# Latent attention: two heads' scores per step, banks by use, and another order in the output projection

## The chip, the core and the metric

The kernel runs on one core of one Trainium2 chip. The metric is the device time in microseconds (us) of one execution of the whole program, lower is better. Engines are named as in the profile: PE (TensorE, matrix products; PEld are its weight loads), DVE (VectorE), ACT (ScalarE), POOL (GpSimd) and SP (SyncE, which here only issues DMAs). Each engine runs its own instructions in the order in which the program gives them and waits on semaphores for the others.

## What is computed

Two blocks follow one another on 512 tokens of width 1024. The first (convolution, stick-breaking attention, gated feed-forward) is not touched. The second has two layers of this form:

```python
for l in range(DEPTH):                                   # DEPTH = 2
    z = rmsnorm(x, norm_g[l]) @ w_in[l]                  # split into the parts of both mixers
    o_gla = gla_mix(...) * silu(g_gate)                  # 4 heads x 128, chunked gated linear attention
    q = (rmsnorm(c_q) @ w_uq[l]).reshape(B, S, 4, 192)   # 128 plain + 64 rotary values per head
    kv = (rmsnorm(c_kv) @ w_ukv[l]).reshape(B, S, 4, 256)
    q, k = rmsnorm per head, rotary on the last 64       # k's rotary part is one for all heads
    o_mla = block_causal_attention(q, k, v) * silu(m_gate)
    x = x + concat([o_gla, o_mla]) @ w_out[l]
```

`block_causal_attention` takes blocks of 128 queries: scores of block i over the keys up to its end, the causal mask on the diagonal block, softmax, product with the values. So for each of 4 heads there are 4 query blocks, with 128, 256, 384 and 512 keys.

## The kernel before

Everything is kept with features on the partitions and tokens along the free dimension: `X` is the residual in 8 blocks of 128 features by 512 tokens. A product with a weight matrix is made of blocks of 128x128 (`block`, L446 is the `mm` inside): each is three passes of 512 columns, high weights by high input, high by low, low by high (`XH`, `XL` are the two parts of an input, `wh`, `wl` those of the weights). `weight_order` writes out the order in which PE uses all weight blocks; they come in units of 8, which SP loads into `wraw`, ACT rounds to `wh` (L1096) and DVE completes with `wl` (L1686). The calls of `feed` and `feed_group` put this work into the queues of ACT and DVE, three units ahead of PE.

The order of all engines is written out by hand. In each layer of the second block, after the values (`by_token`, copied from banks 4 to 7 to `gv` by ACT), PE runs the attention mixed with the first pass of the output projection. Bank numbers are those of PSUM, 8 banks of 128x512.

- `att_scores(j)`, j = 4 * head + query block, on PE: a product with 128 rows (`qraw`, `kraw`; in the trace `bank<-states,gq` or `gk`), one with 64 rows for the rotary part (`qr`, `krh`; in the trace `bank<-krh,eb`), both in fp32, each two passes in the trace, and a mask (`identb`, `mml`). Head parity decides which half of the rows the rotary part uses. DVE takes the negated maximum (L2352) and scales it; ACT makes Exp with its sum (`tmp<-bank,sm,vr`); DVE takes the reciprocal (L2357) and scales the row (L1681).
- `att_turn(j)`: PE transposes the normalised row, 1 to 4 transposes (L1059); ACT copies the result to `PT`.
- `att_out(h)`: PE multiplies the values of head h by `PT` (`bank<-PT,gv`, 8 passes); DVE multiplies by the gate (`tmp<-bank,gates`), ACT and DVE make `XH`, `XL` of it: inputs 4 to 7 of the output projection.
- `halves()`: a generator, the first pass of the output projection. For each of 8 column blocks c it runs inputs 0 to 3; a step is two inputs (6 passes of 512 columns); on DVE, with the second step of c, the sum in the bank is added to `X[c]` (semaphore `out_a`). All engines go through the same generator.

The loop over j = 0 to 18 runs `att_scores(j)`, from j = 6 at every fourth step `att_out`, then `att_turn(j - 2)`, then one step of `halves`. `TURNS` lists scores and turns in their order; both rotate through banks 0 to 3, `att_out` uses banks 6 and 7, `halves` banks 4 and 5 by turns. The queues of ACT and DVE have the same loop.

After it comes the second pass: for each c inputs 4 to 7 (`out_a` and `at_t` free the banks), DVE adds to `X[c]` (`xsum`). In layer 0 ACT and DVE at once prepare the next layer's input from it, in layer 1 SP stores each `X[c]`.

Of the kernel before, what the change touches and what calls it, by code (L numbers as in the profile page):

```python
# [5 lines left out]
ALU = mybir.AluOpType  # L6
# [7 lines left out]
S = 512  # L14
D = 1024
KD = 8
# [29 lines left out]
def weight_order():  # L46
# [29 lines left out]
    for layer in range(2):  # L76
# [12 lines left out]
        o += [(f"out{layer}", k, c) for c in range(8) for k in range(4, KD)]  # L89
# [202 lines left out]
def place(nc, ctx, m):  # L292
# [86 lines left out]
    m.qr, m.kr = m.eb, m.kpb  # L379
    m.qraw = [m.gq[:, 0, :], m.gq[:, 1, :], m.gk[:, 0, :], m.gk[:, 1, :]]  # L380
# [8 lines left out]
TURNS = [("s", 0), ("s", 1)] + [x for j in range(2, 18) for x in ([("s", j)] if j < 16 else []) + [("t", j - 2)]]  # L389
# [52 lines left out]
def tensor_program(pe, m, s, w):  # L442
# [340 lines left out]
    for layer in range(2):  # L783
# [235 lines left out]
        def halves():  # L1019
            for c in range(8):  # L1020
                if c >= 2:
                    pe.wait_ge(s.out_a, 8 * layer + c - 1)
                else:
                    pe.wait_ge(s.gv, 8 * layer + 6)
                for k in range(4):
                    pe.wait_ge(s.mt, 8 * layer + k + 1)
                    block("out" + L, k, c, bank[4 + c % 2][:, :], XH[:, k, :], XL[:, k, :], k == 0, k == 3)
                    if k % 2:
                        yield

        side = halves()
        def free(n):

            if n >= 4:
                kind, j = TURNS[n - 4]
                pe.wait_ge(s.at_p if kind == "s" else s.at_t, 16 * layer + j + 1)
            else:
                pe.wait_ge(s.gate_r, 8 * layer + 8)

        def att_scores(j):  # L1040
            h, qb = j // 4, j % 4
            r = slice(64 * (h % 2), 64 * (h % 2) + 64)
            n, qs = 128 * (qb + 1), slice(qb * 128, qb * 128 + 128)
            t = TURNS.index(("s", j))
            o = bank[t % 4]
            free(t)
            mm(o[:, 0:n], m.qraw[h][:, qs], m.kraw[h][:, 0:n], True, False)
            mm(o[:, 0:n], m.qr[r, h // 2, qs], m.krh[r, h // 2, 0:n], False, False)
            mm(o[:, qs], m.identb[:, :], m.mml[:, :], False, True).then_inc(s.at_s, 1)

        def att_turn(j):
            qb = j % 4
            t = TURNS.index(("t", j))
            o = bank[t % 4]
            free(t)
# [16 lines left out]
        for j in range(19):  # L1072
            if j < 16:
                att_scores(j)
            if j >= 6 and j % 4 == 2:
                att_out((j - 6) // 4)
            if 2 <= j < 18:
                att_turn(j - 2)
            next(side, None)
        for c in range(8):  # L1080
            if c < 2:
                pe.wait_ge(s.out_a, 8 * layer + c + 7)
            elif c < 6:
                pe.wait_ge(s.at_t, 16 * layer + 16)
            else:
                pe.wait_ge(s.xsum, 40 + 8 * layer + c - 5)
            for k in range(4, KD):
                pe.wait_ge(s.mt, 8 * layer + k + 1)
                block("out" + L, k, c, bank[(c + 4) % 6][:, :], XH[:, k, :], XL[:, k, :], k == 4, k == KD - 1)


def scalar_program(act, m, s, w, nc):
# [374 lines left out]
    for layer in range(2):  # L1467
# [164 lines left out]
        def att_scores(j):  # L1632
            qb = j % 4
            n = 128 * (qb + 1)
            o = bank[TURNS.index(("s", j)) % 4]
            act.wait_ge(s.at_m, 16 * layer + j + 1)
            if j >= 3:
                act.wait_ge(s.at_tr, 16 * layer + j - 2)
            c = 96 + 4 * qb + j // 4
            fn(tmp[j % 3][:, 0:n], o[:, 0:n], ACT.Exp, bias=m.sm[:, 3 * j:3 * j + 1], scale=m.vr[:, c:c + 1],  # L1640
               accum_out=m.sm[:, 3 * j + 1:3 * j + 2]).then_inc(s.at_p, 1)

        def att_turn(j):
            h, qb = j // 4, j % 4
            n, qs = 128 * (qb + 1), slice(qb * 128, qb * 128 + 128)
            o = bank[TURNS.index(("t", j)) % 4]
            act.wait_ge(s.at_tr, 16 * layer + j + 1)
            if h:
                act.wait_ge(s.at_o, 4 * layer + h)
            fn(m.PT[:, 0:qb + 1, qs], o[:, 0:n].rearrange("p (k n) -> p k n", n=128), ACT.Copy).then_inc(s.at_t, 1)  # L1650

        for j in range(19):
            if j < 16:
                att_scores(j)
            if j >= 6 and j % 4 == 2:
                h = (j - 6) // 4
                act.wait_ge(s.at_u, 4 * layer + h + 1)
                fn(XH[:, 4 + h, :], tmp[3][:, :], ACT.Copy).then_inc(s.mt_h, 1)
            if 2 <= j < 18:
                att_turn(j - 2)  # L1660
            next(side, None)
        for c in range(8):
# [899 lines left out]
```

## Time and profile before

| | |
|---|---|
| median of 3 runs | 1881.66 us (1878.33 to 1883.82) |
| the profiled execution | 1881.7 us, its span 1879.9 us |
| PE busy | 1819.2 us (97% of the span) |
| DVE busy | 1027.1 us (55%) |
| ACT busy | 819.0 us (44%) |
| mean granted clock of PE | 0.989 |

The span goes from the first to the last instruction of the profiled execution. Busy time of an engine is the union of its instructions; one PE pass overlaps the next in its end. A granted clock of 1.00 is 2.4 GHz, 0.50 is 1.2 GHz. Times in the trace count from the start of the span.

### The profile page before, as it was taken

How to read it: one execution, taken by the hardware profiler on the slowest of the kernel's cores; microseconds unless marked ns; L12 is line 12 of the kernel's file. 1: busy time of each engine (PE TensorE's matmuls, PEld its weight loads, DVE VectorE, ACT ScalarE, POOL GpSimd, SP SyncE). 2: the span in 40 equal slices, each digit the busy share in tenths (PEclk: the TensorE clock that was granted, in tenths of full speed). 3: DMA queues.
4: the chain of work that ended last, by engine and by line, in shares of the span. 5: the costliest groups of instructions: out<-in, count | busy, mean ns of one | idle time of the engine just before them, and what ended most of it. 6: DMA issues, size and time to landing. Idle time of an engine off the chain costs nothing.

```text
span 1879.9 us, 23003 instructions
## 1 busy us (share of the span) xinstructions
PE 1819.2 (97%) x9554; PEld 1462.7 (78%) x9554; DVE 1027.1 (55%) x1565; ACT 819.0 (44%) x1274; POOL 23.9 (1%) x21
## 2 busy tenths in 40 slices
PE   8997899999999999999989999999999999999999
PEld 6886888888888887777678888888877866778666
DVE  5676764544533536776554544533457455556553
ACT  5657653333322345555353333332363253443442
POOL 0000100000000000000100000000000000000000
PEclk9999999999999999999999999999999999999999
DMA  5331222332232231111122332232222211222111
GB/s 200 102 102 45 85 84 90 93 110 90 90 112 92 76 101 56 46 51 62 56 79 90 92 110 90 91 112 91 87 72 85 66 56 45 79 89 80 46 45 45
DMA packets 44199, 154.81 MB, mean 82 GB/s; under 512 B 5024, under 2 KB 5184, under 8 KB 44096
## 3 DMA queue, kind: packets, MB, share of 16 engines
q1 hardware_dynamic: 44096, 153.36, 25.2%
q8 instruction: 75, 1.23, 0.3%
q14 instruction: 28, 0.23, 0.0%
HBM read 150.19 MB, written 2.10 MB: 81 GB/s over the span
## 4 chain that ended last, share of the span: by engine, by line
PE 81%; issue 6%; DVE 6%; ACT 5%; DMA 0%; POOL 0%; POOLq 0%; SPq 0%; DVEq 0%; ACTq 0%
PE bank L446 81%; DVE tmp L1677 1%; DVE wl L1686 1%; ACT wh L1096 1%; ACT XH L1096 1%; ACT tmp L1096 1%; ACT X L1096 1%; ACT Y L1096 0%; PE bank L1059 0%; DVE XL L1686 0%; DVE acc_q L1674 0%; DMA wraw<-in_wstream 0%; ACT L1099 0%; DVE gates L1677 0%; DVE X L1674 0%
## 5 line engine op out<-in xcount | busy, mean ns | idle before, releaser
L446 PE MATMUL bank<-XH,wh 128*128 128x512 f32 (+1 forms) x1680 | 644.2, 383 | 32.0 <-DVE XL L1686 14.7
L446 PE MATMUL bank<-XL,wh 128*128 128x512 f32 (+1 forms) x1680 | 627.6, 374 | 0.0
L446 PE MATMUL bank<-XH,wl 128*128 128x512 f32 (+1 forms) x1680 | 627.3, 373 | 0.0
L1686 DVE TENSOR_TENSOR wl<-wraw,wh 128x1024 fp32r<-128x1024 f32 x278 | 339.2, 1229 | 304.1 <-ACT wh L1096 304.1
L1096 ACT ACTIVATE wh<-wraw 128x1024 fp32r<-128x1024 f32 x278 | 291.4, 1054 | 289.1 <-PE bank L446 282.1
L446 PEld LDWEIGHTS bank<-XH,wh 128*128 128x128 f32 x1680 | 319.7, 190 | 102.3 <-issue 24.3
L446 PEld LDWEIGHTS bank<-XH,wl 128*128 128x128 f32 x1680 | 319.5, 190 | 56.3
L446 PEld LDWEIGHTS bank<-XL,wh 128*128 128x128 f32 x1680 | 320.1, 191 | 54.2 <-issue 2.6
L446 PE MATMUL bank<-HH,wh 128*128 128x512 f32 (+1 forms) x428 | 162.5, 380 | 10.3 <-ACT PP L1096 10.3
L1674 DVE SCALAR_TENSOR_TENSOR tmp<-bank,prm,tmp 128x511 f32<-128x511 f32 x88 | 65.9, 749 | 172.1 <-ACT tmp L1096 170.6
L446 PE MATMUL bank<-HL,wh 128*128 128x512 f32 (+1 forms) x428 | 159.4, 373 | 0.0
L446 PE MATMUL bank<-HH,wl 128*128 128x512 f32 (+1 forms) x428 | 159.2, 372 | 0.0
L1096 ACT ACTIVATE tmp<-bank,prm 128x512 f32<-128x512 f32 (+1 forms) x62 | 45.7, 738 | 195.3 <-PE bank L446 195.1
L446 PEld LDWEIGHTS bank<-HH,wh 128*128 128x128 f32 x428 | 81.7, 191 | 27.7 <-ACT PP L1096 12.7
L446 PEld LDWEIGHTS bank<-HL,wh 128*128 128x128 f32 x428 | 81.8, 191 | 14.7 <-issue 1.2
L446 PEld LDWEIGHTS bank<-HH,wl 128*128 128x128 f32 x428 | 82.0, 192 | 13.8
L1096 ACT ACTIVATE tmp<-tmp 128x512 f32<-128x512 f32 (+1 forms) x65 | 39.4, 605 | 98.6 <-DVE tmp L1674 90.7
L1677 DVE TENSOR_TENSOR X<-X,bank 128x512 f32<-128x512 f32 (+1 forms) x58 | 38.3, 664 | 38.3 <-PE bank L446 38.3
L1096 ACT ACTIVATE sqr<-X 128x512 f32<-128x512 f32 (+1 forms) x39 | 22.7, 586 | 65.6 <-DVE X L1677 61.5
L1677 DVE TENSOR_TENSOR Y<-Y,bank 32x510 f32<-32x510 f32 (+1 forms) x64 | 43.3, 677 | 14.1 <-ACT Y L1096 12.2
L446 PE MATMUL bank<-wh,XH 128*128 128x512 f32 x128 | 50.6, 395 | 0.1
L446 PE MATMUL bank<-wh,XL 128*128 128x512 f32 x128 | 49.9, 389 | 0.0
(285 smaller groups left out, 2092.1 us busy)
## 6 DMA issues: line engine op xcount, KB each, us to landing
wraw<-in_wstream SPq DMA_DIRECT2D x278, 512.0 KB, 3.5
X<-in_xt SPq DMA_DIRECT2D x8, 256.0 KB, 6.4
out<-X SPq DMA_DIRECT2D x8, 256.0 KB, 2.0
pts<-in_pt SPq DMA_DIRECT2D x4, 256.0 KB, 3.7
cst<-in_consts SPq DMA_DIRECT2D x1, 810.0 KB, 9.2
kpa<-lr SPq DMA_DIRECT2D x4, 128.0 KB, 3.9
kpb<-lr SPq DMA_DIRECT2D x8, 64.0 KB, 3.1
acc_s<-in_pos SPq DMA_DIRECT2D x1, 256.0 KB, 4.2
```

The source lines that it names most:

```text
L446: return pe.e.matmul(o, l, r, start=start, stop=stop, skip_group_check=True)
L1096: return act.e.activation(o, i, f, **kw)
L1674: return dve.e.scalar_tensor_tensor(out=o, in0=i0, scalar=sc, in1=i1, op0=op0, op1=op1)
L1677: return dve.e.tensor_tensor(o, i0, i1, op)
L1686: return dve.e.tensor_tensor(o, x, h.bitcast(F32), ALU.subtract)
```

## The change

- Scores: a step n takes two heads of a pair (0 and 1, then 2 and 3) at one query block: both products with 128 rows, then both rotary products one behind the other, in the two halves of the rows and in two banks, then both masks. `HEAD` and `QB` give head and query block of the new index j.
- Banks: 0 to 3 for scores, 4 and 5 for turned rows, 6 for the product with the values, 7 for the first pass of the output projection.
- The turned rows of odd heads go to `gates[0:4]`, of even ones to `PT`. Four buffers `tmp` instead of three; the gated product goes to `sqr` instead of `tmp[3]`.
- A step is: scores of two heads, (in steps 5 and 9 a product), a step of `halves`, (the other product), a turn, a step of `halves`, a turn. DVE has per step: both heads' softmax work, the products' work, then two steps of `halves`.
- Waits: column block c of the first pass waits for the addition of block c - 1 (before: c - 2), the first for all four value copies (before: two).
- Second pass: for columns 0 to 3 first inputs 4 and 5, then 6 and 7; then columns 4 to 7 with all four. The weight stream's order follows.

```diff
@@ -86,7 +86,8 @@
         o += [(f"ukv{layer}", 0, 4 + c) for c in range(4)]
         for c in range(8):
             o += [(f"out{layer}", k, c) for k in range(4)]
-        o += [(f"out{layer}", k, c) for c in range(8) for k in range(4, KD)]
+        o += [(f"out{layer}", k, c) for ks in ((4, 5), (6, 7)) for c in range(4) for k in ks]
+        o += [(f"out{layer}", k, c) for c in range(4, 8) for k in range(4, KD)]
...
+    m.PTs = [m.PT, m.gates[:, 0:4, :]]
...
-TURNS = [("s", 0), ("s", 1)] + [x for j in range(2, 18) for x in ([("s", j)] if j < 16 else []) + [("t", j - 2)]]
+HEAD = [j // 8 * 2 + j % 2 for j in range(16)]
+QB = [j // 2 % 4 for j in range(16)]
+A_SCORES, A_TURN, A_OUT, A_SIDE = [0, 1, 2, 3], [4, 5], 6, 7
...
@@ -1018,75 +1023,79 @@
 
         def halves():
             for c in range(8):
-                if c >= 2:
-                    pe.wait_ge(s.out_a, 8 * layer + c - 1)
+                if c:
+                    pe.wait_ge(s.out_a, 8 * layer + c)
                 else:
-                    pe.wait_ge(s.gv, 8 * layer + 6)
+                    pe.wait_ge(s.gv, 8 * layer + 8)
                 for k in range(4):
                     pe.wait_ge(s.mt, 8 * layer + k + 1)
-                    block("out" + L, k, c, bank[4 + c % 2][:, :], XH[:, k, :], XL[:, k, :], k == 0, k == 3)
+                    block("out" + L, k, c, bank[A_SIDE][:, :], XH[:, k, :], XL[:, k, :], k == 0, k == 3)
                     if k % 2:
                         yield
...
+        def att_scores(n):
+
+            i, qb = n // 4, n % 4
+            w_, qs = 128 * (qb + 1), slice(qb * 128, qb * 128 + 128)
+            o = [bank[A_SCORES[(2 * n + hh) % 4]] for hh in range(2)]
+            if n >= 2:
+                pe.wait_ge(s.at_p, 16 * layer + 2 * n - 2)
             else:
                 pe.wait_ge(s.gate_r, 8 * layer + 8)
-
-        def att_scores(j):
-            h, qb = j // 4, j % 4
-            r = slice(64 * (h % 2), 64 * (h % 2) + 64)
-            n, qs = 128 * (qb + 1), slice(qb * 128, qb * 128 + 128)
-            t = TURNS.index(("s", j))
-            o = bank[t % 4]
-            free(t)
-            mm(o[:, 0:n], m.qraw[h][:, qs], m.kraw[h][:, 0:n], True, False)
-            mm(o[:, 0:n], m.qr[r, h // 2, qs], m.krh[r, h // 2, 0:n], False, False)
-            mm(o[:, qs], m.identb[:, :], m.mml[:, :], False, True).then_inc(s.at_s, 1)
+            for hh in range(2):
+                mm(o[hh][:, 0:w_], m.qraw[2 * i + hh][:, qs], m.kraw[2 * i + hh][:, 0:w_], True, False)
+            for hh in range(2):
+                r = slice(64 * hh, 64 * hh + 64)
+                mm(o[hh][:, 0:w_], m.qr[r, i, qs], m.krh[r, i, 0:w_], False, False)
+            for hh in range(2):
+                mm(o[hh][:, qs], m.identb[:, :], m.mml[:, :], False, True).then_inc(s.at_s, 1)
...
         def att_turn(j):
...
+            o = bank[A_TURN[j % 2]]
+            if j >= 2:
+                pe.wait_ge(s.at_t, 16 * layer + j - 1)
+            else:
+                pe.wait_ge(s.gv, 8 * layer + 8)
             pe.wait_ge(s.at_n, 16 * layer + j + 1)
-            for kb in range(qb + 1):
+            for kb in range(QB[j] + 1):
                 c = slice(kb * 128, (kb + 1) * 128)
-                ins = pe.e.transpose(o[:, c], m.tmp[j % 3][:, c], C("ident"))
+                ins = pe.e.transpose(o[:, c], m.tmp[j % 4][:, c], C("ident"))
             ins.then_inc(s.at_tr, 1)
...
         def att_out(h):
-            o = bank[6 + h % 2]
-            pe.wait_ge(s.at_t, 16 * layer + 4 * h + 4)
+            o = bank[A_OUT]
+            pe.wait_ge(s.at_t, 16 * layer + 8 * (h // 2) + 7 + h % 2)
             pe.wait_ge(s.gv, 8 * layer + 8)
-            if h >= 2:
-                pe.wait_ge(s.at_u, 4 * layer + h - 1)
+            if h:
+                pe.wait_ge(s.at_u, 4 * layer + h)
             for kb in range(4):
-                ins = mm(o[:, kb * 128:S], m.gv[:, kb, h * 128:(h + 1) * 128], m.PT[:, kb, kb * 128:S], kb == 0, kb == 3)
+                ins = mm(o[:, kb * 128:S], m.gv[:, kb, h * 128:(h + 1) * 128], m.PTs[h % 2][:, kb, kb * 128:S], kb == 0, kb == 3)
             ins.then_inc(s.at_o, 1)
 
...
+        for n in range(10):
+            if n < 8:
+                att_scores(n)
+            if n in (5, 9):
+                att_out(n // 4 * 2 - 2)
...
+            if n in (5, 9):
+                att_out(n // 4 * 2 - 1)
+            if 1 <= n < 9:
+                att_turn(2 * n - 2)
+                next(side, None)
+                att_turn(2 * n - 1)
+        for _ in side:
+            pass
+        for cs, ks in ((range(4), (4, 5)), (range(4), (6, 7))) + tuple(((c,), range(4, KD)) for c in range(4, 8)):
+            for c in cs:
+                if c < 6:
+                    pe.wait_ge(s.at_t, 16 * layer + 16)
+                else:
+                    pe.wait_ge(s.xsum, 40 + 8 * layer + c - 5)
+                for k in ks:
+                    pe.wait_ge(s.mt, 8 * layer + k + 1)
+                    block("out" + L, k, c, bank[(c + 4) % 6][:, :], XH[:, k, :], XL[:, k, :], k == 4, k == KD - 1)
...
 
...
+            if j >= 4:
+                act.wait_ge(s.at_tr, 16 * layer + j - 3)
+            c = 96 + 4 * QB[j] + HEAD[j]
+            fn(tmp[j % 4][:, 0:n], bank[A_SCORES[j % 4]][:, 0:n], ACT.Exp, bias=m.sm[:, 3 * j:3 * j + 1],
+               scale=m.vr[:, c:c + 1], accum_out=m.sm[:, 3 * j + 1:3 * j + 2]).then_inc(s.at_p, 1)
...
+            n, qs = 128 * (QB[j] + 1), slice(QB[j] * 128, QB[j] * 128 + 128)
...
+            if j >= 8:
+                act.wait_ge(s.at_o, 4 * layer + j % 2 + 1)
+            else:
+                act.wait_ge(s.mt, 8 * layer + 4)
+            fn(m.PTs[j % 2][:, 0:QB[j] + 1, qs], bank[A_TURN[j % 2]][:, 0:n].rearrange("p (k n) -> p k n", n=128),
+               ACT.Copy).then_inc(s.at_t, 1)
+
+        def att_out(h):
+            act.wait_ge(s.at_u, 4 * layer + h + 1)
+            fn(XH[:, 4 + h, :], sqr[h % 2][:, :], ACT.Copy).then_inc(s.mt_h, 1)
+
+        for n in range(10):
+            if n < 8:
+                att_scores(2 * n)
+                att_scores(2 * n + 1)
+            if n in (5, 9):
+                att_out(n // 4 * 2 - 2)
             next(side, None)
+            if n in (5, 9):
+                att_out(n // 4 * 2 - 1)
+            if 1 <= n < 9:
+                att_turn(2 * n - 2)
+                next(side, None)
+                att_turn(2 * n - 1)
+        for _ in side:
...
@@ -2336,39 +2353,49 @@
                     feed(("out" + L, k, c))
                     if k == 3:
                         dve.wait_ge(s.stream, w.done("out" + L, 3, c))
-                        tt(X[:, c, :], X[:, c, :], bank[4 + c % 2][:, :], ALU.add).then_inc(s.out_a, 1)
+                        tt(X[:, c, :], X[:, c, :], bank[A_SIDE][:, :], ALU.add).then_inc(s.out_a, 1)
                     if k % 2:
                         yield
...
+        def att_scores(n):
+            js, sm = (2 * n, 2 * n + 1), lambda j, i: m.sm[:, 3 * j + i:3 * j + i + 1]
+            w_ = 128 * (QB[2 * n] + 1)
+            for j in js:
+                dve.wait_ge(s.at_s, 16 * layer + j + 1)
+                t = dve.mark(dve.e.reduce_max(sm(j, 0), bank[A_SCORES[j % 4]][:, 0:w_], AX.X, negate=True))
+                dve.wait_ge(dve.own, t)
+                c = 96 + 4 * QB[j] + HEAD[j]
+                tt(sm(j, 0), sm(j, 0), m.vr[:, c:c + 1], ALU.mult).then_inc(s.at_m, 1)
+            for j in js:
+                p = tmp[j % 4][:, 0:w_]
+                dve.wait_ge(s.at_p, 16 * layer + j + 1)
+                t = dve.mark(dve.e.reciprocal(sm(j, 2), sm(j, 1)))
+                dve.wait_ge(dve.own, t)
+                ts(p, p, sm(j, 2), None, ALU.mult).then_inc(s.at_n, 1)
...
+        def att_out(h):
+            t = sqr[h % 2]
+            dve.wait_ge(s.at_o, 4 * layer + h + 1)
+            dve.wait_ge(s.gate, 8 * layer + 5 + h)
+            tt(t[:, :], bank[A_OUT][:, :], m.gates[:, 4 + h, :], ALU.mult).then_inc(s.at_u, 1)
+            dve.wait_ge(s.mt_h, 8 * layer + 5 + h)
+            less(XL[:, 4 + h, :], t[:, :], XH[:, 4 + h, :]).then_inc(s.mt, 1)
+
+        for n in range(10):
+            if n < 8:
+                att_scores(n)
+            if n in (5, 9):
+                att_out(n // 4 * 2 - 2)
             next(side, None)
+            if n in (5, 9):
+                att_out(n // 4 * 2 - 1)
+            if 1 <= n < 9:
+                next(side, None)
+        for _ in side:
```

The queue of ACT has the same order as PE's with two Exp per step, `att_out` as a copy to `XH`, and the turns; its removed lines and some of PE's and DVE's are left out above.

## Rows read from the trace of the kernel before

**Rows 1.** The page: busy time of the engines, and two groups of section 5.

```profile
PE 1819.2 (97%) x9554; PEld 1462.7 (78%) x9554; DVE 1027.1 (55%) x1565; ACT 819.0 (44%) x1274; POOL 23.9 (1%) x21
...
L1686 DVE TENSOR_TENSOR wl<-wraw,wh 128x1024 fp32r<-128x1024 f32 x278 | 339.2, 1229 | 304.1 <-ACT wh L1096 304.1
...
L1096 ACT ACTIVATE wh<-wraw 128x1024 fp32r<-128x1024 f32 x278 | 291.4, 1054 | 289.1 <-PE bank L446 282.1
```

**Rows 2.** Windows, us: length, busy per engine (instructions), clock, DMA share, GB/s; both layers.

```profile
1542.28:1607.40 65.12, 61.39 (x258) 38.66 (x256) 35.56 (x88) 29.11 (x67) 0.00 (x0) 1.00 0.11 33
1790.11:1856.73 66.62, 62.90 (x258) 39.72 (x256) 35.65 (x88) 29.11 (x67) 0.00 (x0) 0.97 0.06 17
```

**Rows 3.** Waits of PE over 1536 to 1608: total, times, longest; layer 0.

```profile
PE bank L446 <- ACT gv L1096: 2.2, 1, 2.2
PE bank L1059 <- DVE tmp L1681: 0.8, 1, 0.8
PE bank L446 <- ACT PT L1096: 0.7, 1, 0.7
```

**Rows 4.** Timeline of PE: start, duration, engine, line, what; scores at 512 and 128.

```profile
1552.73 1.02 PE L446 MATMUL bank<-states,gq 128*128 128x512 f32 x2
...
1553.68 1.12 PE L446 MATMUL bank<-krh,eb 64*128 64x512 f32 x2
...
1554.74 0.23 PE L446 MATMUL bank<-mml,identb 128*128 128x128 bf16 x1
...
1556.42 0.38 PE L446 MATMUL bank<-states,gq 128*128 128x128 f32 x2
...
1556.73 0.49 PE L446 MATMUL bank<-krh,eb 64*128 64x128 f32 x2
...
1557.15 0.23 PE L446 MATMUL bank<-mml,identb 128*128 128x128 bf16 x1
```

**Rows 5.** Timeline of PE, three cuts of one place in the gated scores.

```profile
1714.98 0.37 PE L446 MATMUL bank<-gq,gk 64*128 64x128 f32 x1
...
1714.98 0.38 PE L446 MATMUL bank<-gq,gk 64*128 64x128 f32 x2
...
1714.98 1.16 PE L446 MATMUL bank<-gq,gk 64*128 64x128 f32 x16
```

**Rows 6.** Timeline of all engines, one softmax at 512 columns, then at 128.

```profile
1569.36 0.23 PE L446 MATMUL bank<-mml,identb 128*128 128x128 bf16 x1
...
1569.57 0.49 PE L446 MATMUL bank<-XH,wh 128*128 128x512 f32 x1
...
1569.62 0.69 DVE L2352 TENSOR_REDUCE sm<-bank 128x1 f32<-128x512 f32 x1 [1.45 <-PE bank L446]
...
1570.55 0.78 ACT L1096 ACTIVATE tmp<-bank,sm,vr 128x512 f32<-128x512 f32 x1 [2.93 <-DVE sm L1677]
...
1571.05 0.38 PE L446 MATMUL bank<-states,gk 128*128 128x128 f32 x2
...
1571.44 0.16 DVE L2357 RECIPROCAL sm<-sm 128x1 f32<-128x1 f32 x1 [0.94 <-ACT tmp L1096]
...
1572.05 0.68 DVE L1677 TENSOR_TENSOR X<-X,bank 128x512 f32<-128x512 f32 x1
...
1572.64 0.28 DVE L2352 TENSOR_REDUCE sm<-bank 128x1 f32<-128x128 f32 x1
...
1573.74 0.16 DVE L2357 RECIPROCAL sm<-sm 128x1 f32<-128x1 f32 x1 [0.62 <-ACT tmp L1096]
```

**Rows 7.** Timeline, the value copies at the entry of layer 0.

```profile
1544.32 2.03 ACT L1096 ACTIVATE gv<-bank 128x512 f32<-128x512 f32 x4
```

**Rows 8.** Timeline of PE, one head's product with the values.

```profile
1563.64 2.38 PE L446 MATMUL bank<-PT,gv 128*128 128x512 f32 x8
```

**Rows 9.** Windows of 4 us after the entry of layer 1; columns as above.

```profile
1792.00:1796.00 4.00, 2.73 (x7) 2.15 (x8) 1.58 (x5) 3.97 (x9) 0.00 (x0) 0.65 0.00 0
1796.00:1800.00 4.00, 4.00 (x15) 2.36 (x14) 2.63 (x8) 1.65 (x4) 0.00 (x0) 0.93 0.16 36
```

More of the change, by code:

```diff
@@ L1031, in tensor_program @@
         side = halves()
[L1032 to L1036, printed above, removed]
+        def att_scores(n):
[4 more added lines that the diff above has]
+                pe.wait_ge(s.at_p, 16 * layer + 2 * n - 2)
             else:
@@ L1051, in att_turn @@
-        def att_turn(j):
[L1052 to L1055, printed above, removed]
+            for hh in range(2):
[5 more added lines that the diff above has]
+                mm(o[hh][:, qs], m.identb[:, :], m.mml[:, :], False, True).then_inc(s.at_s, 1)
@@ L1070, in att_out @@
             ins.then_inc(s.at_o, 1)
[L1072 to L1078, printed above, removed]
-            next(side, None)
[L1080 to L1089, printed above, removed]
+        for n in range(10):
[3 more added lines that the diff above has]
+                att_out(n // 4 * 2 - 2)
+            next(side, None)
+            if n in (5, 9):
[4 more added lines that the diff above has]
+                att_turn(2 * n - 1)
@@ L1632, in att_scores @@
         def att_scores(j):
-            qb = j % 4
-            n = 128 * (qb + 1)
-            o = bank[TURNS.index(("s", j)) % 4]
+            n = 128 * (QB[j] + 1)
             act.wait_ge(s.at_m, 16 * layer + j + 1)
[L1637 to L1641, printed above, removed]
+            if j >= 4:
+                act.wait_ge(s.at_tr, 16 * layer + j - 3)
@@ L1643, in att_turn @@
+            c = 96 + 4 * QB[j] + HEAD[j]
+            fn(tmp[j % 4][:, 0:n], bank[A_SCORES[j % 4]][:, 0:n], ACT.Exp, bias=m.sm[:, 3 * j:3 * j + 1],
+               scale=m.vr[:, c:c + 1], accum_out=m.sm[:, 3 * j + 1:3 * j + 2]).then_inc(s.at_p, 1)
         def att_turn(j):
-            h, qb = j // 4, j % 4
-            n, qs = 128 * (qb + 1), slice(qb * 128, qb * 128 + 128)
-            o = bank[TURNS.index(("t", j)) % 4]
+            n, qs = 128 * (QB[j] + 1), slice(QB[j] * 128, QB[j] * 128 + 128)
@@ L1647, in att_turn @@
             act.wait_ge(s.at_tr, 16 * layer + j + 1)
[L1648 to L1660, printed above, removed]
-            next(side, None)
+            if j >= 8:
+                act.wait_ge(s.at_o, 4 * layer + j % 2 + 1)
+            else:
+                act.wait_ge(s.mt, 8 * layer + 4)
@@ L1662, in scalar_program @@
+        for _ in side:
+            pass
         for c in range(8):
@@ L2344, in vector_program @@
         dve.wait_ge(s.hr, 2 * layer + 2)
-        def att_scores(j):
-            qb = j % 4
-            n = 128 * (qb + 1)
-            o, p = bank[TURNS.index(("s", j)) % 4], tmp[j % 3]
-            nm, sumr, rc = (m.sm[:, 3 * j + i:3 * j + i + 1] for i in range(3))
-            dve.wait_ge(s.at_s, 16 * layer + j + 1)
-            t = dve.mark(dve.e.reduce_max(nm, o[:, 0:n], AX.X, negate=True))
-            dve.wait_ge(dve.own, t)
-            c = 96 + 4 * qb + j // 4
-            tt(nm, nm, m.vr[:, c:c + 1], ALU.mult).then_inc(s.at_m, 1)
-            dve.wait_ge(s.at_p, 16 * layer + j + 1)
-            n1 = dve.mark(dve.e.reciprocal(rc, sumr))
-            dve.wait_ge(dve.own, n1)
-            ts(p[:, 0:n], p[:, 0:n], rc, None, ALU.mult).then_inc(s.at_n, 1)
@@ L2361, in vector_program @@
-        for j in range(19):
-            if j < 16:
-                att_scores(j)
-            if j >= 6 and j % 4 == 2:
-                h = (j - 6) // 4
-                dve.wait_ge(s.at_o, 4 * layer + h + 1)
-                dve.wait_ge(s.gate, 8 * layer + 5 + h)
-                tt(tmp[3][:, :], bank[6 + h % 2][:, :], m.gates[:, 4 + h, :], ALU.mult).then_inc(s.at_u, 1)
-                dve.wait_ge(s.mt_h, 8 * layer + 5 + h)
-                less(XL[:, 4 + h, :], tmp[3][:, :], XH[:, 4 + h, :]).then_inc(s.mt, 1)
-            next(side, None)
+        def att_scores(n):
[13 more added lines that the diff above has]
+                ts(p, p, sm(j, 2), None, ALU.mult).then_inc(s.at_n, 1)
@@ L2372, in vector_program @@
+        for _ in side:
+            pass
         for c in range(8):
```

## Prediction, made before the changed kernel was run

> **What bounds the kernel now.** I read the page first: TensorE (PE) is busy for 97% of the span, the other engines for about half [rows 1]. So only PE's own work, or a wait that PE meets, can move the time. Next the two stretches that the change touches, the attention with the first pass of the output projection, one in each layer: 65.12 us in layer 0 and 66.62 in layer 1, with PE busy all but 3.7 us [rows 2]. The table of waits names those 3.7 us: 2.2 at the entry (for ScalarE's copies of the values), 0.8 and 0.7 at the end (last turned rows, last copy to PT), the same in both layers [rows 3]. Between entry and end PE never waits. There is thus little idle time to win, 16 steps of PE work to shorten, and no slack that PE itself needs. Layer 1 is 1.5 us longer with the same work because its clock was at half for a while [rows 2, 9].
>
> **Rotary scores side by side (the gain).** Each head's score is two full-row passes (states), two 64-row passes (krh), and the mask. At 512 columns the krh part runs from 1553.68 to 1554.74, 1.06 us; at 128 columns from 1556.73 to 1557.15, 0.42 [rows 4]. The states part takes 0.95 and 0.31, so 384 columns more cost 0.64, 128 columns 0.21, and 0.10 of each is the switch into 64 rows. The four widths are evenly spaced: four heads' blocks of one head cost 4 x (0.42 + 1.06)/2 + 4 x 0.10 = 3.36 us. Do two adjacent heads, in opposite halves of the rows, share this time? The kernel has the same form elsewhere, fp32 with 64 rows, alternating halves, two banks: the second pass starts within 0.01 us of the first, and 16 passes of 128 columns last 1.16 us in all [rows 5], where at krh's 0.2 us a pass they would be 3.4. So one of two heads' krh parts vanishes: two pairs of heads per layer, 2 x 3.36 = 6.7 us a layer, 13.4 in both. The mask (0.07) and the full-row passes stay. Bounds: nothing shared, 0; shared for one pass of two, about 9; I take 13.3, since the row is the same pattern.
>
> The Trainium skill (TensorEngine Tiling (Array Packing), Key Properties) says that changing the tiling mode drains TensorE; the 0.10 us at each switch agrees. Its section PSUM Bottleneck of the same page says that tiling speeds up TensorE but not the emptying of PSUM, which may become the bottleneck. That speaks against this change, and the next part finds the same from the queues.
>
> **One bank for the first output pass (the loss).** Before, column block c of the first pass went to bank 4 + c%2 and waited only for block c-2's addition. Now all eight use bank 7, and block c waits for VectorE's addition of block c-1 (out_a >= c). Place this in the queues of step n (1 to 7). PE: scores of two heads, second half of block c = n-1, a turn, first half of block n, a turn. VectorE: all of att_scores(n), and only then the addition of block n-1. So the first half of block n can't begin until the whole softmax of the two heads just scored is through VectorE, with both Exp of ScalarE between, plus the addition. Queued behind that wait on PE are the second turn and the scores of n+1, and VectorE and ScalarE then wait for those: a closed loop.
>
> Its length from the mask of the first head, at 512 columns [rows 6]: mask to reduce 0.26, reduce to reciprocal 1.82, one more Exp with its read for the second head 0.87 (1570.55 to 1571.44, less the handoff), reciprocal to the next operation 0.61, addition 0.68 and handoff 0.05: 4.3 us. At 128 columns reduce to reciprocal is 1.10, the second head and the scaling are shorter: 3.0. In between 3.4 and 3.85. PE covers meanwhile: mask 0.1, half a block 1.48 (1569.57 to 1571.05), and the turn, 0.11 for each of its 1 to 4 transposes (two plus the mask are 0.21): 1.7 to 2.0 us. Stalls: step 2 (384) 2.0, step 3 (512) 2.3, step 4 (128) 1.0, step 6 2.0, step 7 2.3. Step 1 (256) 1.7, and about 1 more, as VectorE first does its 1.23 us rest of a weight unit, after ScalarE's 1.05 [rows 1], and ScalarE's first Exp is late there as it was: 2.7. Step 5 has both products of the first two heads (2.4 us each, [rows 8]) around the half block, which cover the loop: 0. Sum 12.3 us a layer, 24.6 in both. Bounds: if my handoffs are 0.4 us too long at each of the 12 stalls, 20; if too short by as much, 29.
>
> **The entry.** The first half block waited for the second of four value copies, now for the fourth: two more at 0.51 each [rows 7], 1.0 us later. Into that wait goes the second head's full-row score and mask, 0.28. Loss 0.7 a layer, 1.4 in all.
>
> **The end.** Before, PE waited 0.8 + 0.7 with no filler left, and some 0.25 before input 7 of block 0. Now there is still a half block at step 8, the last turns have old data, and out(2) waits some 0.25 for a copy. But heads 2 and 3 share bank 6: out(3) waits for VectorE's product of out(2), as long as an addition, 0.7, with handoffs 1.0. So 1.75 becomes 1.25, gain 0.5 a layer, 1.0 in all. **The second pass** does the same 32 blocks; inputs 4 and 5 of four columns (8 blocks, 5.5 us) cover the way of heads 2 and 3 to XH and XL (0.7 + 0.6 + 0.7). Without that cover it would cost about 0.3 a layer, as it did. The additions of columns 0 to 2 come some 4 us later and bunch on VectorE before layer 1's input; inputs 4 to 7 of it are needed only 11 us into it, so 0, at most 1. DMAs: the stream's order changes, not its size; the weights are three units ahead. One slot's rounding is asked for earlier and waits for its free slot, with ScalarE having nothing urgent behind it: 0. The last column and its store stay last.
>
> **The clock.** The 2.2 us wait at the entry of layer 1 was followed by a fall of the granted clock (2.4 GHz to 1.2): 0.65 and 0.93 over two stretches of 4 us are (0.35 + 0.07) x 4 / 0.5 = 3.4 us at half, and the stage came out 1.5 longer [rows 2, 9]. The same wait in layer 0 did not do it. One fall for two such waits; the change has 12 waits near 2 us or above (the entry and five steps, in each layer). I'd expect 6 falls; as some of the slow time lies in the cover of a later stall, I count 5, at 1.4 each, less the one of before: +5.5. Bounds: no more than before, 0, and ten, +13.
>
> **Sum.** The profiled execution took 1881.7 us, its span 1879.9 with 1.8 around it, equal to the median of 1881.66. 1881.7 - 13.3 + 24.6 + 1.4 - 1.0 + 5.5 = 1898.9, taken as 1899. About 0.3% (5.6 us) is what a measurement of this kernel tells from no change.
>
> **Rivals.**
> (a) The same loop, clock no worse than before: 1893.4. It is inside the forecast's case; for it, layer 0's wait without a fall; against, the number of waits.
> (b) Faster: the addition is in time. The gain per layer is 6.7 and six steps stall, so the point is a mean stall of 1.1 us. It needs VectorE's and ScalarE's part to overlap so far that the loop is 3 us at every width. Without any stall and without layer 1's fall: 1881.7 - 13.3 + 1.4 - 1.0 - 1.5 = 1867. Against it: the addition stands behind both heads' scaling in VectorE's queue, and 1.82 + 0.87 us of that are read off rows. Chance 0.09.
> (c) Even: handoffs shorter, stalls near 1.2 us: 14 + 0.4 against 13.3, some 1883. Chance 0.10.
> (d) The pair doesn't run side by side, each head's passes queue behind each other: the gain goes and the loop stays: 1899 + 13 = 1912; half of it, 1903. Against it [rows 5]. It also is the case in which the change doesn't do what it says. Chance 0.07.
> The forecast's own case has 0.74. Range: 1886 to 1909, from stalls 4.6 less and no further fall (1889, and 3 towards (c)) to 0.3 us more at each of 12 stalls and eight falls (1907, and 2 towards (d)). Slower by over 0.3% (above 1887.3): 0.80; within: 0.11; faster: 0.09.
>
> **What would show it.** After: krh passes in pairs 0.01 us apart; PE waiting for VectorE's X (the addition) some 12 times, 1 to 2.7 us each, 20 to 29 us in sum, none in step 5; one wait for the product of out(2) in each layer; the 0.8 us wait for turned rows gone; clock below 1.00 in both stretches. The first to fail would be the loop's length: if the waits for X sum to under 12 us, the forecast is wrong and (b) or (c) holds.

## The result, and the profile after

The changed kernel took 1902.83 us (median of 5 runs, 1899.97 to 1905.48), the kernel before 1879.15 beside it: slower by 1.15% (ratio on record 1.0115, 95% interval 1.0099 to 1.0131; these two medians lie 23.7 us apart). The forecast was 1899, with a range of 1886 to 1909.

The page, engines and clock:

```profile
span 1903.0 us, 23011 instructions
...
PE 1821.4 (96%) x9554; PEld 1469.6 (77%) x9554; DVE 1028.0 (54%) x1565; ACT 820.1 (43%) x1274; POOL 23.9 (1%) x21
```

The same number of passes, hardly more busy time than in [rows 1], and a span 23.1 us longer. PE waits more, and what the pairs save in its busy time is used up by passes at the slow clock. The waits of PE in layer 0 (total, times, longest):

```profile
PE bank L451 <- DVE X L1694: 10.3, 6, 2.2
PE bank L451 <- ACT gv L1105: 2.9, 1, 2.9
PE bank L451 <- DVE sqr L1694: 0.9, 1, 0.9
...
PE bank L451 <- ACT PT L1105: 0.3, 1, 0.3
```

Against [rows 3] six waits for `X`, VectorE's addition, are new; the entry (`gv`) is 0.7 longer; the 0.8 us for turned rows is gone, the last copy's wait 0.3 instead of 0.7; one wait for the product of a head (`sqr`) has come. Layer 1 has the same 10.3 us. The stretch from the first score to the output's second pass, in windows of both layers, first of the kernel after (length, PE, PEld, DVE, ACT, POOL busy, clock, DMA share, GB/s):

```profile
1543.91:1617.20 73.29, 58.99 (x249) 38.93 (x248) 34.65 (x86) 27.83 (x65) 0.00 (x0) 0.93 0.09 30
1801.90:1877.79 75.89, 61.56 (x250) 40.55 (x248) 34.64 (x86) 27.85 (x65) 0.00 (x0) 0.89 0.04 14
```

then of the kernel before, cut at the same instructions:

```profile
1542.28:1604.99 62.71, 59.08 (x250) 37.08 (x248) 34.18 (x86) 27.70 (x65) 0.00 (x0) 1.00 0.11 34
1790.11:1854.32 64.21, 60.57 (x250) 38.13 (x248) 34.27 (x86) 27.70 (x65) 0.00 (x0) 0.97 0.06 17
```

The stretches are 10.6 and 11.7 us longer, 22.3 of the 23.1. The clock column is the second thing to see. What the mean lacks to 1.00, divided by the 0.5 that a slow microsecond lacks, gives the time at half clock: 0.07 x 73.29 / 0.5 = 10 us in layer 0 and 0.11 x 75.89 / 0.5 = 17 in layer 1, against none and some 3.5 before.

One turn of the loop, step 3 of layer 0 (512 columns), PE and the others in order of time:

```profile
1567.22 1.13 PE L451 MATMUL bank<-krh,eb 64*128 64x512 f32 x4
1568.29 0.29 PE L451 MATMUL bank<-mml,identb 128*128 128x128 bf16 x2
...
1568.55 0.69 DVE L2368 TENSOR_REDUCE sm<-bank 128x1 f32<-128x512 f32 x1 [3.68 <-PE bank L451]
...
1569.84 0.49 PE L1063 MATMUL bank<-cst,tmp 128*128 128x128 f32 x3
...
1570.27 0.78 ACT L1105 ACTIVATE tmp<-bank,sm,vr 128x512 f32<-128x512 f32 x1
...
1571.37 0.49 DVE L1698 TENSOR_SCALAR tmp<-tmp,sm 128x512 f32<-128x512 f32 x1
1571.77 0.68 DVE L1694 TENSOR_TENSOR X<-X,bank 128x512 f32<-128x512 f32 x1
1572.51 0.59 PE L451 MATMUL bank<-XH,wh 128*128 128x512 f32 x1 [2.17 <-DVE X L1694]
```

The rotary passes of two heads (x4) run from 1567.22 to 1568.29, 1.07 us, where one head alone took 1.06 [rows 4]. From the masks to the next half block it is 4.22 us (1568.29 to 1572.51), by way of the second Exp, the second scaling and the addition. PE's own work had ended at 1570.34.

### The profile page after: what moved, and what is told of

It is laid out like the page before. It is cut to its first block, busy times and chain, and to the rows that moved or that the text cites. A ratio compares the mean times of both kernels' runs of the same rounds, so it can differ in the third digit from the quotient of the medians.

```text
span 1903.0 us, 23011 instructions
## 1 busy us (share of the span) xinstructions
PE 1821.4 (96%) x9554; PEld 1469.6 (77%) x9554; DVE 1028.0 (54%) x1565; ACT 820.1 (43%) x1274; POOL 23.9 (1%) x21
## 4 chain that ended last, share of the span: by engine, by line
PE 80%; DVE 7%; issue 6%; ACT 6%; DMA 0%; POOL 0%; POOLq 0%; SPq 0%; DVEq 0%; ACTq 0%
PE bank L451 80%; ACT tmp L1105 1%; DVE wl L1703 1%; DVE tmp L1694 1%; ACT wh L1105 1%; ACT XH L1105 1%; ACT X L1105 1%; DVE X L1694 0%; DVE tmp L1698 0%; DVE acc_q L1691 0%; DVE sm L2368 0%; ACT Y L1105 0%; PE bank L1063 0%; ACT L1108 0%; DVE gates L1694 0%
## 5 line engine op out<-in xcount | busy, mean ns | idle before, releaser
L451 PE MATMUL bank<-XH,wh 128*128 128x512 f32 (+1 forms) x1680 | 647.1, 385 | 53.4 <-DVE X L1694 20.6
L451 PE MATMUL bank<-HH,wh 128*128 128x512 f32 (+1 forms) x428 | 163.2, 381 | 10.3 <-ACT PP L1105 10.3
L451 PE MATMUL bank<-wl,XH 128*128 128x512 f32 x128 | 49.8, 389 | 0.0
```

The lines of the kernel that those rows point to most:

```text
L451: return pe.e.matmul(o, l, r, start=start, stop=stop, skip_group_check=True)
```

## The experiments

**Theory**: the loss is a closed loop, PE to VectorE's softmax of both heads to the addition and back, made by one side bank together with the place of the addition; the clock's falls come on top; the rotary gain is there all the while. **Rivals**: two heads in one piece are too long for VectorE with any banks; the pair gains nothing; the slow clock lies in time that PE waits anyway.

**1. Two side banks.** One bank moved from the turned rows to the first output pass:

```diff
-A_SCORES, A_TURN, A_OUT, A_SIDE = [0, 1, 2, 3], [4, 5], 6, 7
+A_SCORES, A_TURN, A_OUT, A_SIDE = [0, 1, 2, 3], [4, 4], 6, [5, 7]
...
-                if c:
-                    pe.wait_ge(s.out_a, 8 * layer + c)
+                if c >= 2:
+                    pe.wait_ge(s.out_a, 8 * layer + c - 1)
                 else:
-                    pe.wait_ge(s.gv, 8 * layer + 8)
+                    pe.wait_ge(s.gv, 8 * layer + 6 + 2 * c)
...
-            if j >= 2:
-                pe.wait_ge(s.at_t, 16 * layer + j - 1)
+            if j:
+                pe.wait_ge(s.at_t, 16 * layer + j)
...
```

The edit also gives the first half block its old wait back, for two value copies instead of four.

> The changed kernel with one bank moved: turned rows use bank 4 alone, the first output pass alternates between banks 5 and 7, so that column block c waits for the addition of block c-2 again, as before the change. Everything else, the pairs and VectorE's order too, stays. Theory (the loss is the closed loop through the single bank): PE's waits for the addition, 10.3 us idle in each layer, are gone, and with them most falls of the clock; the rotary gain of 6.6 us a layer remains; about 1866 us, faster than before the change by 0.7%. Rival (two heads' work in one piece of VectorE's queue is itself too long, whatever the banks): the waits come back as waits for normalised rows or for the addition of c-2, and the time stays above 1890.

Measured: 1865.61 us, ratio to the kernel before 0.9917 (0.9896 to 0.9938). PE's waits in layer 0, and the stretch:

```profile
PE bank L451 <- ACT gv L1107: 1.9, 1, 1.9
PE bank L451 <- DVE sqr L1696: 0.9, 1, 0.9
PE bank L1063 <- ACT PT L1107: 0.7, 1, 0.7
```

```profile
1537.62:1595.70 58.08, 54.49 (x250) 36.27 (x248) 34.55 (x86) 27.72 (x65) 0.00 (x0) 0.97 0.11 37
```

No wait for `X` is left, and this layer takes 15.2 us less than in the changed kernel. 10.3 us of that is idle time in the loop, 1.0 the shorter wait at the entry (1.9 for 2.9), which is not the loop's, and most of the rest fewer falls of the clock. VectorE's busy time is that of the changed kernel: two heads in one piece are not too long for it. The theory holds, the first rival falls.

**2. The pair undone** in the kernel of experiment 1:

```diff
             for hh in range(2):
                 mm(o[hh][:, 0:w_], m.qraw[2 * i + hh][:, qs], m.kraw[2 * i + hh][:, 0:w_], True, False)
-            for hh in range(2):
                 r = slice(64 * hh, 64 * hh + 64)
                 mm(o[hh][:, 0:w_], m.qr[r, i, qs], m.krh[r, i, 0:w_], False, False)
```

> The kernel with two side banks, with one thing undone: the rotary products of the two heads no longer stand one behind the other (full-row and rotary product of the first head, then of the second). Theory (the pair shares its time): each of 16 pairs costs one krh part more, 6.6 us a layer, 13.3 us in all over the kernel with two side banks, some 1879. Rival (the rotary products gain nothing by standing side by side, the gain is from another step): the same time within 2 us.

Measured: 1881.58 us, ratio to before 0.9995 (0.9982 to 1.0007). The stretch:

```profile
1538.19:1602.98 64.79, 61.81 (x249) 38.07 (x248) 34.63 (x86) 27.72 (x65) 0.00 (x0) 0.97 0.10 33
```

64.79 against 58.08, at the same mean clock: undoing the pair costs 6.7 us a layer. PE's busy time differs by more, 7.3 us (61.81 for 54.49); 0.6 of it goes into the wait at the entry, which is 1.3 us here and 1.9 with the pair. Without the pair the other parts of experiment 1 bring nothing: the time is that of the kernel before, and the stretches are 2.1 and 0.6 us longer than its own. The medians say 16.0 us for the pair; the stretches, 13.5 in both layers, are the better measure, as the last section tells.

**3. The stalls filled.** Needless passes in the changed kernel, before PE's wait:

```diff
                 if c:
+                    if c >= 6:
+                        pe.wait_ge(s.at_u, 4 * layer + 2)
+                    for _ in range((0, 6, 7, 8, 2, 0, 7, 8)[c]):
+                        mm(bank[A_OUT][:, :], XH[:, 0, 0:128], XH[:, 0, :], True, True)
                     pe.wait_ge(s.out_a, 8 * layer + c)
```

> The changed kernel, with 38 passes of 512 columns more on PE in each layer: needless products into the free bank 6 just before PE waits for the addition (6, 7, 8, 2, 7, 8 passes for column blocks 1, 2, 3, 4, 6, 7), less than the waits last. Their results are never read. The loop stays. Theory (the falls of the clock follow the stalls and cost about half of their length, 12 us in both layers): the clock stays up except perhaps at the two entries, and the kernel is 8 to 12 us faster than the changed one, 1891 to 1895, although it does more work. Rival (the slow stretches lie in time that PE waits anyway): no faster than 1903, or slower by what the added passes stick out.

Measured: 1894.98 us, ratio to before 1.0055 (1.0037 to 1.0072), 7.9 below the changed kernel by the medians; the two ratios to the kernel before have intervals that do not touch. The same step 3 of layer 0, with the eight added passes where PE stood, and both stretches:

```profile
1570.90 2.09 PE L451 MATMUL bank<-XH 128*128 128x512 f32 x8
1573.30 0.50 PE L451 MATMUL bank<-XH,wh 128*128 128x512 f32 x1 [0.31 <-DVE X L1698]
```

```profile
1544.71:1614.82 70.11, 64.58 (x288) 43.04 (x286) 34.65 (x86) 27.86 (x65) 0.00 (x0) 0.98 0.09 31
1799.48:1869.02 69.54, 63.01 (x288) 42.06 (x286) 34.55 (x86) 27.85 (x65) 0.00 (x0) 1.00 0.05 16
```

More work, 3.2 and 6.3 us shorter, the clock at 0.98 and 1.00. The loop itself has kept its length (mask 1569.08 to half block 1573.30 is 4.22 again). So the falls of the clock cost real time, 9.5 us at least in both layers. Those behind the loop's stalls come from the stalls: the changed kernel has 5 of them, the same loop in experiment 6 also 5, this kernel none. The waits at the entries were not filled. One of them is still followed by a fall, in layer 0; in layer 1 none follows, where the changed kernel has its longest. Up to 1.6 of the 9.5 us are therefore not the filling's, but chance of this execution (from the first half block to that of step 1, layer 1 takes 7.46 us here and 9.08 in the changed kernel).

**4. The addition between maxima and reciprocals**, with one side bank:

```diff
         def att_scores(n, between=lambda: None):
...
                 tt(sm(j, 0), sm(j, 0), m.vr[:, c:c + 1], ALU.mult).then_inc(s.at_m, 1)
+            between()
             for j in js:
...
+            early = n in (1, 2, 3, 4, 6, 7)
             if n < 8:
-                att_scores(n)
+                att_scores(n, (lambda: next(side, None)) if early else (lambda: None))
...
-            next(side, None)
+            if not early:
+                next(side, None)
```

> The changed kernel with the single side bank kept, and only VectorE's order changed: in steps 1, 2, 3, 4, 6 and 7 the addition of the column block comes after the two maxima and before the two reciprocals. Theory (the loop is long because the addition stands behind the whole softmax of both heads): from the mask the addition is through after 2.5 to 2.7 us instead of 2.9 to 4.2, PE's waits for it fall from 10.3 us a layer to 3 to 5, and with fewer falls of the clock the time is about 1881 (1876 to 1887). Rival (one bank is too few in any order): the waits stay near 10 us a layer, or come back as waits for normalised rows, and the time is above 1895.

Measured: 1881.45 us, ratio to before 0.9992 (0.9975 to 1.0009). VectorE in step 3 of layer 0:

```profile
1567.33 0.69 DVE L2368 TENSOR_REDUCE sm<-bank 128x1 f32<-128x512 f32 x1
1568.05 0.16 DVE L1694 TENSOR_TENSOR sm<-sm,vr 128x1 f32<-128x1 f32 x1
1568.12 0.68 DVE L1694 TENSOR_TENSOR X<-X,bank 128x512 f32<-128x512 f32 x1
1568.72 0.16 DVE L2376 RECIPROCAL sm<-sm 128x1 f32<-128x1 f32 x1
```

PE's waits for it:

```profile
PE bank L451 <- DVE X L1694: 3.2, 6, 0.7
```

The order of two operations in one queue takes 7.1 of the 10.3 us away with the bank still single. Bank and order are thus two halves of one cause: the second bank takes the waits away wholly, the order by itself two thirds of them.

**5. One side bank alone**, in the kernel before:

```diff
-                if c >= 2:
-                    pe.wait_ge(s.out_a, 8 * layer + c - 1)
+                if c:
+                    pe.wait_ge(s.out_a, 8 * layer + c)
...
-                    block("out" + L, k, c, bank[4 + c % 2][:, :], XH[:, k, :], XL[:, k, :], k == 0, k == 3)
+                    block("out" + L, k, c, bank[4][:, :], XH[:, k, :], XL[:, k, :], k == 0, k == 3)
...
```

> The kernel before the change with one part of it alone: the first output pass uses bank 4 only, so that column block c waits for the addition of block c-1. Heads one at a time, order of all queues as before. Theory (the loop needs the bank and the two heads together): between the mask of an odd step and the next block's first half PE has a turn, half a block, another score and another turn, 2.9 to 3.4 us, against 2.8 to 3.4 us of VectorE's and ScalarE's work with the addition; only 1 to 3 us of waits a layer, the time 2 to 6 us above before. Rival (one bank costs its 20 us in any schedule): waits for the addition of 10 us a layer, 1900 or more.

Measured: 1888.15 us, ratio to before 1.0024 (1.0012 to 1.0036). PE's waits in layer 0 besides those of [rows 3]:

```profile
PE bank L446 <- DVE X L1677: 2.7, 4, 1.4
```

In layer 1 it is 1.3 us. The stretches are 3.9 and 2.3 us longer than those of the kernel before. One bank alone thus costs a quarter of what it costs with the two heads; that the score of another head lies between is the reason I see in the order of the queues.

**6. The old order of the second pass** in the changed kernel (the two lines of the weight order and the loop of the diff undone), one profiled execution:

> The changed kernel with the old order of the output's second pass (each column with inputs 4 to 7 at once, and the weight stream in that order). Theory (the new order covers the way of heads 2 and 3 to XH and XL, worth 0.3 us a layer): between the end of the second product and the end of the span 0.3 us more in layer 1 than the changed kernel's, and a short wait of PE before input 7 of the first column; the time of the whole is within the spread. Rival (the order matters more, or not at all): over 1 us a layer, or under 0.1.

Measured: 1901.66 us, within the spread of the changed kernel. From the end of the second product to the end of the span, first with the old order, then the changed kernel:

```profile
1874.26:1899.90 25.64, 22.38 (x99) 17.85 (x97) 8.01 (x11) 1.58 (x2) 0.00 (x0) 1.00 0.21 82
```

```profile
1877.79:1903.00 25.21, 22.02 (x99) 17.91 (x97) 8.12 (x11) 1.58 (x2) 0.00 (x0) 1.00 0.22 84
```

0.4 us where 0.3 was expected, the smallest part of the change. The expected short wait before input 7 is there: its first pass starts 0.48 us behind the one before it (1876.20 to 1876.68), where 0.23 is usual. The bunched additions cost nothing: from the end of that stretch to the first score of layer 1 it is 184.7 us with the new order (1617.20 to 1801.90), 185.1 before.

**7. The other waits moved** in the kernel of experiment 1: out(3) to bank 3, turn 15 to bank 0, and the scores of step 1 ahead of the first half block:

```diff
-            o = bank[A_TURN[j % 2]]
+            o = bank[A_TURN[j % 2] if j < 15 else 0]
...
-            o = bank[A_OUT]
+            o = bank[A_OUT if h < 3 else 3]
...
-            if n < 8:
+            if n == 0:
+                att_scores(0)
+                att_scores(1)
+            elif 2 <= n < 8:
                 att_scores(n)
...
```

> The kernel with two side banks, and its three last waits of PE per layer attacked: the last product and the last turned row go to score banks that are free by then (3 and 0), so that neither waits for VectorE's product nor for ScalarE's copy, and PE scores the second step's heads before its first half block, inside the wait for the value copies. Theory (each wait of the trace is real and nothing stands behind it): 0.9 and 0.7 us gone, 1.3 or more of the entry's 1.9 filled, less up to 0.4 of a new wait for the first normalised rows: 2.5 to 3.3 us a layer, 1859 to 1861 against 1865.6. Rival (they only make room for the next wait): within 1 us of 1865.6.

Measured: 1871.34 us, ratio to before 0.9943 (0.993 to 0.9955). The median lies above what theory and rival allowed, but by the stretch the rival is right: 57.86 us against 58.08. (The median of experiment 1's own kernel is 1870.59 in experiment 9.) Where the gain went, in PE's waits of layer 0:

```profile
PE bank L1065 <- ACT PT L1117: 2.3, 1, 2.3
PE bank L1065 <- DVE tmp L1710: 0.4, 1, 0.4
```

All three waits went, but for 0.2 us at the entry, and PE now met turn 1 earlier, in the one bank 4, from which ScalarE takes turn 0 only after both Exp of step 1, which stand behind VectorE's rest of a weight unit. My expectation had allowed for the first normalised rows (0.4, as it came) but not for the queue of the copy.

**8. Odd turned rows in bank 6** where it is free of products, on top of 7:

```diff
-            o = bank[A_TURN[j % 2] if j < 15 else 0]
+            o = bank[4 if j % 2 == 0 or j == 9 else 0 if j == 15 else 6]
             if j == 15:
                 pe.wait_ge(s.at_p, 16 * layer + 16)
-            elif j:
+            elif j in (9, 10):
                 pe.wait_ge(s.at_t, 16 * layer + j)
+            elif j >= 2:
+                pe.wait_ge(s.at_t, 16 * layer + j - 1)
...
```

> The kernel all_waits_moved, with odd turned rows in bank 6, where it is free of a head's product (not turn 9 and 15), so that turn 1 no longer waits for ScalarE's copy of turn 0. Theory (the 2.3 us wait of PE for that copy took the place of the waits removed): the stretch from the first score to the second output pass falls from 57.9 us by 1.5 to 2.3 us, both layers 3 to 5 us. Rival (VectorE's rest of a weight unit and ScalarE's order hold PE at the next point instead): under 1 us a layer.

Measured: 1863.23 us, ratio to before 0.9893 (0.9879 to 0.9906), the fastest of all. What PE still waits for in layer 0, and both stretches:

```profile
PE bank L1069 <- DVE tmp L1714: 0.4, 1, 0.4
PE bank L451 <- DVE vr L1710: 0.3, 1, 0.3
PE bank L451 <- ACT PT L1121: 0.2, 1, 0.2
```

```profile
1545.36:1599.07 53.71, 52.77 (x249) 35.18 (x248) 34.23 (x86) 27.49 (x65) 0.00 (x0) 1.00 0.12 40
1783.78:1837.47 53.69, 52.77 (x249) 35.16 (x248) 34.23 (x86) 27.50 (x65) 0.00 (x0) 1.00 0.06 20
```

4.2 us a layer less than experiment 7, where I had expected 1.5 to 2.3: with the 2.3 us wait went the stretch at half clock that had followed it, some 3.5 us long and worth 1.7 in each layer (the mean clock is 0.97 there and 1.00 here, PE's busy time 54.63 us there and 52.77 here).

**9. Experiment 1 once more**, beside 8:

> The kernel two_side_banks once more, on the same chip and beside the same runs of the kernel before as turns_in_two_banks. Theory (6 us between executions come from falls of the clock in the first 1540 us, which no kernel here changes): its stretch again 58.1 us in each layer, its median between 1863 and 1871. Rival (the first result was special): stretch or median outside of these.

Measured: 1870.59 us, ratio to before 0.9931 (0.9917 to 0.9944). The median is 5 us above that of the first time, yet inside the bounds. The stretch, and PE's waits for copies of turned rows (one, of 0.7 us, in experiment 1; two here, one of them new):

```profile
1543.17:1601.02 57.85, 53.10 (x250) 35.04 (x248) 34.52 (x86) 27.76 (x65) 0.00 (x0) 1.00 0.11 37
```

```profile
PE bank L1063 <- ACT PT L1107: 1.8, 2, 1.1
```

In experiment 1 the clock fell at the entry of each layer; here, behind the same wait of 1.9 us, it did not fall. PE worked 1.4 us less (53.10 for 54.49), and yet the stretch is only 0.2 us shorter: PE came to turn 1 earlier and stood there for 1.1 us, at the place where experiment 7 found its 2.3. So a wait near 2 us need not be followed by a fall, and a fall just ahead of a wait can cost next to nothing. Beside it on one chip experiment 8 is 7.4 us faster.

## Why the prediction was right

Step by step, the forecast and what was measured, us for both layers:

| step | forecast | measured | from |
|---|---|---|---|
| rotary scores side by side | -13.3 | -13.5 to -14.6 | experiments 1 and 2, stretches and busy time |
| stalls of the loop | +24.6 | +22.6 | 20.6 idle, and 12 x 0.17 (below) |
| entry | +1.4 | +1.4 | 2.9 for 2.2, twice |
| end, second pass with it | -1.0 | -1.4 | 0.9 + 0.3 for 0.8 + 0.7, and 0.4 a layer |
| falls of the clock | +5.5 | +8.6 to +11.3 | experiment 3; half of the slow time (below) |
| before the stretch, untouched code | 0 | +1.6 | 1543.91 for 1542.28 |
| whole | +17.2 | +23.1 | the spans |

The measured terms, with 11.3 for the clock, add up to 21 or 22 us; 1 to 2 us I can't place. The sign and the mechanism were foreseen. That 1899 came within 4 us of the median is in part luck: the change cost 23.7 us where 17.2 was forecast, but the kernel before came out 2.5 us faster (1879.15) than in the measurement that the forecast started from, and 2 us too much for the stalls made up for a part of what the clock was short.

**The loop** went as it was walked: 4.22 us at 512 columns where 4.3 had been said, six stalls in each layer and none in step 5. Single stalls, idle: 1.52, 1.83, 2.17, 0.78, 1.83, 2.15, against 2.7, 2.0, 2.3, 1.0, 2.0, 2.3 from start to start. To compare, 0.17 belongs to each, the tail of the last transpose (an x1 of them lasts 0.27 and is followed after 0.11 when nothing waits). Only step 1 was shorter than set, by 1 us, and that is the clock's doing: it fell after the entry, PE reached the masks of step 1 later (1552.72), and VectorE's rest of the weight unit, which I had put in the way, was done by then. In layer 1 of experiment 6, which has the same loop and no fall behind that entry, step 1 has its full length:

```profile
1811.51 0.50 PE L450 MATMUL bank<-XH,wh 128*128 128x512 f32 x1 [2.54 <-DVE X L1693]
```

With the 0.17 it is 2.7 us, as forecast. Experiments 1 and 4 show the mechanism from both sides, 5 that it needs both parts.

**The pair** shares its time fully: rival (d) is out by experiment 2 and by the krh rows. The forecast's 6.7 us a layer is what experiment 2 gives by the stretch; against the kernel before, where nothing of the pair hides in the entry's wait, the busy time's 7.3 is the fairer figure. **The end** has its new wait for the product of out(2), 0.9 where 1.0 was said.

**The clock** is the term that was mis-sized. Mechanism and sign held: waits near 2 us are often followed by stretches at 1.2 GHz. I had read one fall for two such waits off [rows 2, 9], expected 6 of the usual 3.4 us, and took off one of them and something of each for slow time that would lie in a later stall's cover. There were 3 in layer 0 and 4 in layer 1, one of these twice as long, 27 us in all where the kernel before has 3.4.

Two readings bound what these falls cost. By the slow time: 1.2 of the 27 us lie in the wait at layer 1's entry, so PE worked some 26 us at half clock, and (26 - 3.4) / 2 = 11.3. By experiment 3: its layer 1, without any fall, takes 69.54 us, and the changed kernel's stretches are 3.8 and 6.4 us longer than that; less the 1.5 us that the fall cost before, 8.6. The difference is cover. A fall behind the entry was covered in part, as I had expected: experiment 3's layer 0, with that one fall, is only 0.6 us longer than its layer 1. The falls behind the loop's stalls were hardly covered (two of them, 6.8 us at half clock, made layer 0 of the changed kernel 3.2 us longer than in experiment 3): PE's work behind a stall, the half block, the turn and the next scores, is itself a part of the loop. So the forecast's 6 falls were near (experiment 6 had 6, 20.5 us in all; the changed kernel 7, and the long one counts double), but it took off too much for cover.

**Rivals.** (a), the loop with no worse clock, 1893.4, is nearly experiment 3 (1894.98): the loop alone makes the kernel slower. (b), no stall at all, said 1867; experiment 1 builds it with the second bank (1865.61). (c), short stalls, said 1883; experiment 4 builds it with the order (1881.45, that is 0 against before). Neither is what the changed kernel does.

The Trainium skill's rule of the forecast (TensorEngine Tiling (Array Packing), PSUM Bottleneck) pointed the right way, but not by the amount of work: emptying the banks took hardly more engine time than before (VectorE 34.65 us for 34.18 in the stretch). What became the bound was the distance from a score to the emptying of another bank.

## What to carry to other kernels

When work is paired or made coarser, follow each buffer with one copy: find the instruction that frees it, and see what stands ahead of it in its engine's queue. A closed loop shows when that instruction is queued behind work which itself waits for the engine that wants the buffer; it costs its whole length per step, however idle both engines are, and is mended by a second buffer or by moving the freeing instruction ahead of the dependent half. A wait removed is worth its length only if the next one is not in the same place: of 3.3 us of waits removed in experiment 7 only 0.2 us was gained, until one more bank was split.

## What the runs showed of the hardware

Stalls of about 2 us on TensorE can cost more than their length. The changed kernel's two stretches held 27 us at half clock, and the kernel with needless passes in its stalls is faster by 7.9 us in the median (9.5 us in the stretches, of which up to 1.6 are chance). Busy work in a gap is not always waste. It is no rule for each single gap: the changed kernel had 12 gaps of 1.5 to 2.9 us in the two stretches and 7 falls, the wait of 1.9 us at the entry was followed by a fall in experiment 1 and by none in experiment 9, and in experiment 2 the clock fell behind one of only 1.3 us.

The falls also make the spread. All kernels here run the same instructions up to the first score of layer 0, yet it began between 1537.62 us (experiment 1) and 1545.36 (experiment 8). The mean clock over one stretch ahead of it, first of experiment 1, then of 8:

```profile
100.00:1530.00 1430.00, 1389.92 (x7276) 1144.08 (x7272) 775.52 (x1138) 624.68 (x950) 20.42 (x14) 0.99 0.26 83
```

```profile
100.00:1530.00 1430.00, 1389.60 (x7250) 1144.24 (x7247) 771.84 (x1134) 624.37 (x949) 20.41 (x14) 0.98 0.25 83
```

PE is idle for the same 40 us in both, so what differs is the pace of its passes. Read in windows of 1 us, 34 us of the first and 48 us of the second are at half clock. That is 7 us of work, and the starts are 7.7 us apart. A stretch cut at the same two instructions, with its own clock beside it, tells a change of 2 us from none (58.08 us at 0.97 and 57.85 at 1.00 for the same kernel), where the medians of that kernel lie 5 us apart.
